# A chunked delta recurrence on one core: key and beta in one 128-row tile, state and outputs as products over 128 stacked rows, and the values' part of the right-hand side taken a chunk ahead

## Chip, cores and metric

One Trainium2 chip, one core, one launch. The metric is the device time of the launch in microseconds, the median of several executions; lower is better.

## What is computed

A decoder layer for 1024 tokens of width 1024 in float32: an RWKV-7 group of 8 heads and an attention group of 8 heads side by side, then a mixing product, LayerNorm, a feed-forward part and LayerNorm. The change touches only the state recurrence of the RWKV group. Cut to what matters:

```python
def wkv7_scan(r, w, k, v, kk, a):
    def step(S, inp):                       # S: 8 heads x 64 x 64
        r_t, w_t, k_t, v_t, kk_t, a_t = inp
        sa = einsum('bhvk,bhk->bhv', S, -kk_t)
        S = (S * w_t[:, :, None, :] + sa[..., :, None] * (kk_t * a_t)[:, :, None, :]
             + v_t[..., :, None] * k_t[:, :, None, :])
        return S, einsum('bhvk,bhk->bhv', S, r_t)
    ...                                     # 1024 steps, one after the other
```

## The kernel before

The launch is a row of blocks, each ended by a barrier of all engines: input projection, attention (`mla`), recurrence (`rwkv_chunks`), and then one long block for the group's outputs, the mixing and the feed-forward part. The order of work on every engine is written out by hand; engines meet only at semaphores, and each engine and each DMA queue runs its instructions in the order of the code.

The recurrence goes over NC_ = 16 chunks of CH = 64 tokens. Within a chunk the 64 steps are solved at once. Eight heads lie as RT = 4 tiles (index c) of 128 partitions, two heads p = 0, 1 to a tile, head p on the partitions `own[p]` (0 to 63 or 64 to 127). So nearly every product is a 64x64 by 64x64 float32 matmul, issued for p = 0 and p = 1 in turn, 8 of them (4 pairs) for one matrix per head. For chunk n the steps on TensorE are:

- `first_product` and the second `product` (L1794): two products that finish the inverse of a triangular matrix, from tiles that SP loads (L1685, six DMAs of 64 KB per chunk). Between them ACT copies out (`product_out`, L1847), and after them DVE merges (`merged`, L1914).
- `scores_step` (L1757, L1760, L1763): undecayed key by kk, undecayed key by decayed r, beta by decayed r, 12 pairs. DVE masks them out of PSUM (`mask_step`, L1923 and L1925).
- `transposes` (L1776, L1779, L1788): beta, key and values turned to token rows by matmuls with a 64-wide identity, 12 pairs. ACT copies them out (`tokens_step`, L1863, L1864).
- `rhs_step` (L1706, L1709): right-hand side, values' part plus state's part summed in PSUM, 8 pairs; DVE copies it (`rhs_out`, L1900).
- `sa_step` (L1718): inverse by right-hand side, 4 pairs; ACT copies it to `u` (`u_step`, L1853).
- `state_step` (L1728, L1731): keys by values plus beta by `u`, 8 pairs; DVE adds and decays (`state_out`, L1904, L1908).
- `y_step` (L1739, L1742, L1745): three products summed in PSUM, 12 pairs; ACT copies out (`y_leave`, L1857).

ACT also makes the decays of the next chunks (`exp_step`), DVE the decayed r (`r_step`), POOL the undecayed key (L1977). Steps of chunk m that need no state run a chunk ahead, between those of chunk n = m - 1:

```python
def stage(m, chain, ahead):
    n, z = m - 1, m % 3
    if ahead and m > 1: first_product(m)
    if chain: rhs_step(n)
    if ahead and m: scores_step(m)
    if chain: sa_step(n)
    ...                                     # second product, transposes(m)
    if chain:
        state_step(n)
        y_step(n)
```

Beta, 2 MB for all tokens, is loaded whole into `beta_all` near the end of the attention block (L1099). SP's queue in the recurrence is: the first quarter of the values (L1673), the six tiles of chunks 1 and 2, then, behind `sa_step(0)`, three quarters of the values and the gate weights, then the tiles of chunk 3, and from there six tiles a chunk, each set behind the `sa_step` three chunks back.

## Time and profile before

| | us |
|---|---|
| median of 3 runs | 1356.23 (1355.48 to 1357.2) |
| the profiled execution, its own time | 1353.33 |
| its span, first to last instruction | 1351.5 |
| recurrence block, first matmul to the first matmul behind it | 470.95 to 605.57 |

In a profile, PE is TensorE's matmuls and PEld its weight loads, DVE is VectorE, ACT is ScalarE, POOL is GpSimd, SP the queue that issues DMAs. L12 is line 12 of the kernel. A float32 matmul of this kernel leaves two records; a pair (p = 0 and p = 1) leaves four. A matmul's record lasts longer than the matmul keeps the engine, since neighbours overlap: pace is read from the starts. "x16" is a count of records; the name in square brackets behind a row is what ended the engine's idle time before it.

### The profile page before, as it was taken

The numbers are of one execution on the slowest core, as the hardware profiler recorded it, in microseconds if no ns is written. First come the engines' busy times: TensorE is split into PE (matmuls) and PEld (weight loads), VectorE is DVE, ScalarE is ACT, GpSimd is POOL, SyncE is SP. The second block draws the span as 40 slices with busy tenths as digits, with TensorE's granted clock in tenths as the row PEclk, the third lists the DMA queues.
The fourth block names the chain that finished last, engine by engine and source line by source line (L and its number), as shares of the span: only waits on it lengthen the run. The fifth ranks groups of instructions, "written<-read, shape, count | busy, mean of one in ns | idle before, by whom it ended". The sixth has DMA issues, their size and how long they took to land.

```text
span 1351.5 us, 23894 instructions
## 1 busy us (share of the span) xinstructions
PE 1315.0 (97%) x9900; PEld 1071.2 (79%) x9900; DVE 945.5 (70%) x1110; ACT 474.8 (35%) x796; POOL 497.0 (37%) x323
## 2 busy tenths in 40 slices
PE   7999999999999989989999999999999999999997
PEld 6877677877776789986688878888888888888886
DVE  3657975257777634439677988877777787669877
ACT  3143643146555433334104522212222444333330
POOL 0000112001876210002084778766774354444030
PEclk9999999999999999999999999999999999999999
DMA  5111444779639952224222345444436986666562
GB/s 225 62 48 32 141 157 156 184 169 292 183 101 288 221 127 53 59 64 140 87 101 94 117 137 198 142 147 164 156 125 226 356 288 219 190 198 200 190 205 106
DMA packets 147372, 214.50 MB, mean 159 GB/s; under 512 B 79960, under 2 KB 86240, under 8 KB 146624
## 3 DMA queue, kind: packets, MB, share of 16 engines
q1 hardware_dynamic: 146976, 211.92, 49.3%
q8 instruction: 79, 1.29, 0.4%
q10 hardware_dynamic: 288, 1.05, 0.2%
q14 instruction: 29, 0.24, 0.1%
HBM read 137.89 MB, written 66.39 MB: 151 GB/s over the span
## 4 chain that ended last, share of the span: by engine, by line
PE 49%; DVE 3%; POOL 1%; issue 1%; ACT 1%; DVEq 0%; POOLq 0%; ACTq 0%
PE banks L2523 23%; PE banks L2410 18%; PE banks L2326 5%; PE banks L2398 2%; POOL tile_h L3083 1%; PE banks L2371 1%; DVE wout_lo L2736 0%; POOL tile_s L3083 0%; DVE y_all L2756 0%; DVE first_relu L2870 0%; PE banks L2352 0%; DVE gn_scale L2747 0%; PE banks L156 0%; PE banks L2337 0%; DVE yr_full L2762 0%
## 5 line engine op out<-in xcount | busy, mean ns | idle before, releaser
L2523 PE MATMUL banks<-stage_b_hi,stage_a_hi 128*128 128x512 f32 x448 | 174.3, 389 | 0.0
L2523 PE MATMUL banks<-stage_b_lo,stage_a_hi 128*128 128x512 f32 x448 | 174.3, 389 | 0.0
L2523 PE MATMUL banks<-stage_b_hi,stage_a_lo 128*128 128x512 f32 x448 | 174.3, 389 | 0.0
L2898 DVE TENSOR_TENSOR stage_a_lo<-stage_a_raw,stage_a_hi 128x1024 fp32r<-128x1024 f32 x56 | 97.7, 1745 | 35.2 <-ACT stage_a_hi L2665 35.2
L2665 ACT ACTIVATE stage_a_hi<-stage_a_raw 128x1024 fp32r<-128x1024 f32 x56 | 59.4, 1061 | 120.9 <-DMA stage_b_raw<-in_w_ffn 98.4
L2523 PEld LDWEIGHTS banks<-stage_b_lo,stage_a_hi 128*128 128x128 f32 x448 | 84.1, 188 | 17.6
L2523 PEld LDWEIGHTS banks<-stage_b_hi,stage_a_hi 128*128 128x128 f32 x448 | 84.1, 188 | 17.4
L2523 PEld LDWEIGHTS banks<-stage_b_hi,stage_a_lo 128*128 128x128 f32 x448 | 84.1, 188 | 17.3
L852 POOL TENSOR_TENSOR hT<-hT,rate 128x1024 f32<-128x1024 f32 x4 | 13.5, 3370 | 210.1 <-DVE kk_tile L773 210.1
L428 PE MATMUL banks<-xT_hi,win_hi 128*128 128x512 f32 x288 | 90.6, 396 | 0.0
L428 PE MATMUL banks<-xT_lo,win_hi 128*128 128x512 f32 x288 | 88.8, 389 | 0.0
L428 PE MATMUL banks<-xT_hi,win_lo 128*128 128x512 f32 x288 | 88.7, 389 | 0.0
L1347 ACT ACTIVATE probs<-banks,neg_row_max 128x512 f32<-128x512 f32 (+1 forms) x96 | 55.3, 581 | 63.9 <-DVE neg_row_max L1442 38.9
L1439 DVE TENSOR_REDUCE row_max_parts<-banks 128x1 f32<-128x512 f32 (+1 forms) x96 | 50.6, 552 | 33.1 <-PE banks L1212 17.8
L428 PEld LDWEIGHTS banks<-xT_hi,win_hi 128*128 128x128 f32 x288 | 53.1, 188 | 19.4 <-issue 8.2
L3107 POOL TENSOR_TENSOR w_slots<-stage_b_raw,w_slots 128x1024 f32<-128x1024 f32 x16 | 45.6, 2856 | 52.9 <-DMA stage_b_raw<-in_w_ffn 48.3
L428 PEld LDWEIGHTS banks<-xT_lo,win_hi 128*128 128x128 f32 x288 | 54.1, 188 | 11.4
L428 PEld LDWEIGHTS banks<-xT_hi,win_lo 128*128 128x128 f32 x288 | 54.1, 188 | 11.3
L2901 DVE TENSOR_TENSOR stage_b_lo<-stage_b_raw,stage_b_hi 128x1024 fp32r<-128x1024 f32 x34 | 53.5, 1574 | 0.4
L1225 PE MATMUL banks<-ident,probs 128*128 128x128 f32 x288 | 48.4, 287 | 4.6 <-ACT late_probs_t L1359 2.5
L1977 POOL TENSOR_TENSOR k_undecayed<-hT,undecay 128x256 f32<-128x256 f32 x15 | 11.1, 743 | 108.3 <-ACT undecay L1841 108.3
L2883 DVE SCALAR_TENSOR_TENSOR tile_h<-tile_h 128x512 f32<-128x512 f32 x56 | 47.6, 849 | 1.4
(423 smaller groups left out, 3590.1 us busy)
## 6 DMA issues: line engine op xcount, KB each, us to landing
stage_b_raw<-in_w_ffn SPq DMA_DIRECT2D x50, 512.0 KB, 5.0
stage_a_raw<-hid_s SPq DMA_DIRECT2D x32, 512.0 KB, 4.0
w_landed<-in_w_ffn SPq DMA_DIRECT2D x30, 512.0 KB, 4.7
hid_s<-tile_s SPq DMA_DIRECT2D x60, 256.0 KB, 4.4
stage_a_raw<-hid_h SPq DMA_DIRECT2D x24, 512.0 KB, 4.0
hid_h<-tile_h SPq DMA_DIRECT2D x42, 256.0 KB, 2.0
win_raw<-in_w_in SPq DMA_DIRECT2D x20, 512.0 KB, 3.6
x_tok<-in_x SPq DMA_DIRECT2D x8, 512.0 KB, 7.6
```

What stands on the lines that cost most here:

```text
L428: last = mm(ps[:, 2 * j + b, :], w[j][:, kt, :], r[:, kt, b * HALF:(b + 1) * HALF], start=kt == 0 and i == 0, stop=kt == KT - 1 and i == 2)
L1225: last = nc.tensor.transpose(ps[:, BANK_T + u % 2, j * P:(j + 1) * P], probs[n % 3][:, j * P:(j + 1) * P], ident[:])
L1347: A_(probs[n % 3][:, 0:width], ps[:, u % 4, 0:width], ACT.Exp, bias=bias[:, qt:qt + 1], scale=SCALE, accum_out=sums[:, m, qt:qt + 1]).then ...
L1439: step.mark(V.reduce_max(tops[:, m, qt:qt + 1], ps[:, u % 4, 0:blocks_of(i, u) * P], AX_X))
L2326: last = nc.tensor.matmul(ps[:, bank + b, :], a[:, kt % RT, tok], w[:, kt, b * HALF:(b + 1) * HALF], start=kt == W_ORDER[0] and n == 0, st ...
L2410: last = nc.tensor.matmul(ps[:, bank_of(u, name), :], a[:, j, cut], b(kt), start=kt == 0 and n == 0, stop=kt == HK - 1 and n == 2)
L2523: last = nc.tensor.matmul(ps[:, bank, :], s[a][:, j, tok], s[b][:, j, :], start=p == 0 and j == 0 and n == 0, stop=p == NP - 1 and j == 1 ...
L2665: A(s["a_hi"][:], s["a_raw"][:], COPY).then_inc(hi2, 1)
L2883: V.scalar_tensor_tensor(hid[name][:], hid[name][:], 0.0, hid[name][:], ALU.max, ALU.mult).then_inc(hid_done, 1)
L2898: V.tensor_tensor(s["a_lo"][:], s["a_raw"][:], s["a_hi"][:].bitcast(F32), ALU.subtract).then_inc(lo2, 1)
L2901: V.tensor_tensor(s["b_lo"][:], src, s["b_hi"][:].bitcast(F32), ALU.subtract).then_inc(lo2, 1)
L3107: G.tensor_tensor(dst, a, b, ALU.subtract).then_inc(combined, 1)
```

## The change

Key and beta now lie in one tile `kb` of 128 partitions x 4 x 2 x 64. Four 128x128 transposes turn both for both heads of a tile at once (L1799 of the changed kernel); in the turned tile `kb_tok` the 64 token rows of the key lie on partitions 0 to 63 and those of beta on 64 to 127. In the same way `vu` holds the values' token rows on partitions 0 to 63 and the solved `u` on 64 to 127, and `rb` the scores of key and of beta by r. So `state_step` is one product over 128 stacked rows per head (8 matmuls of 128x64 weights), and so is the part of `y_step` that comes from values and `u`; the part from the old state stays a 64x64 product, into another bank, and DVE adds the two (`y_sum`), after ACT has copied one. The values' part of the right-hand side becomes `base_step(m)`, run at the end of the stage before; ACT copies it out (`base_out`), and `rhs_out` on DVE becomes an addition of it and the state's part. For the rows to stack, the score, `sa` and value-transpose products of the two heads now write the same 64 output partitions in two neighbouring banks. `beta_all` and its load are gone; chunk 0's beta (128 KB) is loaded in the attention block instead, and SP loads 128 KB of beta for each chunk behind that chunk's six tiles, and the three late quarters of the values also wait for `y_step(0)`. The core of the diff:

```diff
-    bk_tok = new("bk_tok", [P, 2, RT, CH], copies=2)
-    v_tok = new("v_tok", tile, copies=2)
-    u = new("u", tile)
+    kb_tok = new("kb_tok", [P, RT, 2, CH], copies=2)
+    vu = new("vu", [P, 2, RT, CH], copies=2)
...
-    own = (slice(0, 64), slice(64, P))
-    B, K, A_, R = 0, 1, 0, 1
-    B_SA, B_RY, B_T1, B_X, B_KS, B_B, B_BKT, B_V = range(8)
-    Y0 = RT
+    own = key_rows, beta_rows = (slice(0, 64), slice(64, P))
+    B_RY, B_TX, B_SC, _, B_VU, _, B_KB, B_ST = range(8)
+    K, B = 0, 1
+    Y0 = X0 = A0 = RT
     cols = lambda c: slice(c * CH, (c + 1) * CH)
     view = lambda bank, n=RT, at=0: ps[:, bank, at * CH:(at + n) * CH].rearrange("p (c n) -> p c n", n=CH)
+    by_head = lambda bank, rows=slice(0, P), at=0: ps[rows, bank:bank + 2, at * CH:(at + RT) * CH]
...
+                    sp.wait_ge(y_mm, 1)
...
+                if m >= 2:
+                    sp.wait_ge(tr_done, m - 1)
+                sp.dma_start(kb[m % 2][:, :, B, :], k.beta_d[:, :, now(m)]).then_inc(beta_in[m % 2], 16)
...
         def _(pe):
             mm = nc.tensor.matmul
 
-            def rhs_step(n):
-                q, a = n % 2, n % 3
+            def base_step(n):
+                q = n % 2
                 pe.wait_ge(sc_ready, n + 1)
                 pe.wait_ge(v_ready, n + 1)
-                pe.wait_ge(state_ready, n + 1)
-                if n >= 1:
-                    pe.wait_ge(y_out, n)
                 for c in range(RT):
                     for p in range(2):
-                        mm(ps[own[p], B_RY, cols(c)], ks[q][own[p], c, A_, :], v_tok[q][own[p], c, :],
-                           start=True, stop=False)
+                        last = mm(ps[own[p], B_SC, cols(c)], ka[q][key_rows, p, c, :], vu[q][key_rows, p, c, :],
+                                  start=True, stop=True)
+                last.then_inc(base_mm, 1)
+
+            def rhs_step(n):
+                q = n % 2
+                pe.wait_ge(state_ready, n + 1)
+                for c in range(RT):
                     for p in range(2):
-                        last = mm(ps[own[p], B_RY, cols(c)], kk_all[own[p], c, now(n)], state[q][own[p], c, :],
-                                  start=False, stop=True)
+                        last = mm(ps[own[p], B_ST, cols(A0 + c)], kk_all[own[p], c, now(n)], state[q][own[p], c, :],
+                                  start=True, stop=True)
                 last.then_inc(rhs_mm, 1)
 
             def sa_step(n):
                 pe.wait_ge(rhs_ready, n + 1)
                 pe.wait_ge(xt_up, n + 1)
+                if n >= 1:
+                    pe.wait_ge(part_ready, n)
                 for c in range(RT):
                     for p in range(2):
-                        last = mm(ps[own[p], B_SA, cols(c)], inv_t[n % 3][own[p], c, :], rhs[own[p], c, :],
+                        last = mm(ps[beta_rows, B_VU + p, cols(c)], inv_t[n % 3][own[p], c, :], rhs[own[p], c, :],
                                   start=True, stop=True)
                 last.then_inc(sa_mm, 1)
 
...
                 pe.wait_ge(sa_ready, n + 1)
                 for c in range(RT):
                     for p in range(2):
-                        mm(ps[own[p], B_SA, cols(c)], bk_tok[q][own[p], K, c, :], v_tok[q][own[p], c, :],
-                           start=True, stop=False)
-                    for p in range(2):
-                        last = mm(ps[own[p], B_SA, cols(c)], bk_tok[q][own[p], B, c, :], u[own[p], c, :],
-                                  start=False, stop=True)
+                        last = mm(ps[own[p], B_ST, cols(c)], kb_tok[q][:, c, p, :], vu[q][:, p, c, :],
+                                  start=True, stop=True)
                 last.then_inc(s_mm, 1)
 
             def y_step(n):
                 q, a = n % 2, n % 3
+                if n >= 1:
+                    pe.wait_ge(y_out, n)
                 for c in range(RT):
                     for p in range(2):
-                        mm(ps[own[p], B_RY, cols(Y0 + c)], state[q][own[p], c, :], rd[a][own[p], c, :],
-                           start=True, stop=False)
+                        mm(ps[own[p], B_RY, cols(c)], vu[q][:, p, c, :], rb[q][:, p, c, :], start=True, stop=True)
+                if n < NC_ - 1:
+                    pe.wait_ge(v_ready, n + 2)
+                for c in range(RT):
                     for p in range(2):
-                        mm(ps[own[p], B_RY, cols(Y0 + c)], v_tok[q][own[p], c, :], ks[q][own[p], c, R, :],
-                           start=False, stop=False)
-                    for p in range(2):
-                        last = mm(ps[own[p], B_RY, cols(Y0 + c)], u[own[p], c, :], bs[q][own[p], c, :],
-                                  start=False, stop=True)
+                        last = mm(ps[own[p], B_VU, cols(Y0 + c)], state[q][own[p], c, :], rd_of(n)[own[p], c, :],
+                                  start=True, stop=True)
                 last.then_inc(y_mm, 1)
 
             def scores_step(m):
                 q, a = m % 2, m % 3
                 if m >= 1:
                     pe.wait_ge(kd_ready, m)
+                    pe.wait_ge(beta_in[q], 16 * ((m + 1) // 2))
                     pe.wait_ge(rd_ready, m)
                     pe.wait_ge(sc_ready, m)
+                    pe.wait_ge(base_ready, m)
                 for c in range(RT):
                     for p in range(2):
-                        mm(ps[own[p], B_KS, cols(2 * c + A_)], kd[q][own[p], c, :], kk_all[own[p], c, now(m)],
+                        mm(ps[key_rows, B_SC + p, cols(A0 + c)], kb[q][own[p], c, K, :], kk_all[own[p], c, now(m)],
                            start=True, stop=True)
                     for p in range(2):
-                        mm(ps[own[p], B_KS, cols(2 * c + R)], kd[q][own[p], c, :], rd[a][own[p], c, :],
+                        mm(ps[key_rows, B_SC + p, cols(c)], kb[q][own[p], c, K, :], rd_of(m)[own[p], c, :],
                            start=True, stop=True)
                     for p in range(2):
-                        last = mm(ps[own[p], B_B, cols(c)], beta[own[p], c, now(m)], rd[a][own[p], c, :],
+                        last = mm(ps[beta_rows, B_SC + p, cols(c)], kb[q][own[p], c, B, :], rd_of(m)[own[p], c, :],
                                   start=True, stop=True)
                 last.then_inc(scores_mm, 1)
 
             def transposes(m):
                 q = m % 2
+                if m == 0:
+                    pe.wait_ge(centred, 1)
+                if m == 1 or m and m % 4 == 0:
+                    pe.wait_ge(v_in[m // 4], 16)
                 if m >= 1:
                     pe.wait_ge(tok_ready, m)
                 else:
...
                     pe.wait_ge(early_left, 1)
                 for c in range(RT):
                     for p in range(2):
-                        mm(ps[own[p], B_BKT, cols(B * RT + c)], beta[own[p], c, now(m)], k.eye[own[p], :],
-                           start=True, stop=True)
-                    for p in range(2):
-                        mm(ps[own[p], B_BKT, cols(K * RT + c)], kd[q][own[p], c, :], k.eye[own[p], :],
-                           start=True, stop=True)
-                if m == 0:
-                    pe.wait_ge(centred, 1)
-                if m == 1 or m and m % 4 == 0:
-                    pe.wait_ge(v_in[m // 4], 16)
+                        v = hT[own[p], T_V + c, now(m)] if m else k.first_v[own[p], c, :]
+                        mm(ps[key_rows, B_VU + p, cols(c)], v, centre[own[p], :], start=True, stop=True)
                 for c in range(RT):
-                    for p in range(2):
-                        v = hT[own[p], T_V + c, now(m)] if m else k.first_v[own[p], c, :]
-                        last = mm(ps[own[p], B_V, cols(c)], v, centre[own[p], :], start=True, stop=True)
+                    last = nc.tensor.transpose(ps[:, B_KB, c * P:(c + 1) * P],
+                                               kb[q][:, c, :, :].rearrange("p a n -> p (a n)"), ident[:])
                 last.then_inc(tr_done, 1)
 
...
+                pe.wait_ge(xt_up, m)
+                product(B_TX, low_t[z], inv[z]).then_inc(t1_mm, 1)
...
+                if ahead:
+                    base_step(m)
...
             def u_step(n):
                 act.wait_ge(sa_mm, n + 1)
-                if n >= 1:
-                    act.wait_ge(y_mm, n)
-                A(u[:], view(B_SA), ACT.Copy).then_inc(sa_ready, 1)
+                A(vu[n % 2][beta_rows, :, :, :].rearrange("p a c n -> p a (c n)"), by_head(B_VU, beta_rows), ACT.Copy)\
+                    .then_inc(sa_ready, 1)
 
             def y_leave(n):
                 act.wait_ge(y_mm, n + 1)
-                A(y_all[:, :, now(n)], view(B_RY, at=Y0), ACT.Copy).then_inc(y_out, 1)
+                if n >= 1:
+                    act.wait_ge(y_out, n)
+                A(y_part[:], view(B_VU, at=Y0), ACT.Copy).then_inc(part_ready, 1)
+
+            def base_out(n):
+                act.wait_ge(base_mm, n + 1)
+                if n >= 1:
+                    act.wait_ge(rhs_ready, n)
+                A(base[:], view(B_SC), ACT.Copy).then_inc(base_ready, 1)
 
             def tokens_step(m):
                 act.wait_ge(tr_done, m + 1)
                 if m >= 2:
                     act.wait_ge(y_mm, m - 1)
-                A(v_tok[m % 2][:], view(B_V), ACT.Copy).then_inc(v_ready, 1)
-                A(bk_tok[m % 2][:].rearrange("p a c n -> p (a c) n"), view(B_BKT, 2 * RT), ACT.Copy)\
-                    .then_inc(tok_ready, 1)
-
-            A(k.att_q[0][:], ps[:, B_BKT, :], ACT.Copy).then_inc(late_left, 1)
+                A(vu[m % 2][key_rows, :, :, :].rearrange("p a c n -> p a (c n)"), by_head(B_VU, key_rows), ACT.Copy)\
+                    .then_inc(v_ready, 1)
+                A(kb_tok[m % 2][:].rearrange("p c a n -> p (c a n)"), ps[:, B_KB, :], ACT.Copy).then_inc(tok_ready, 1)
...
             def rhs_out(n):
                 dve.wait_ge(rhs_mm, n + 1)
+                dve.wait_ge(base_ready, n + 1)
                 if n >= 1:
                     dve.wait_ge(sa_mm, n)
-                V.tensor_copy(rhs[:], view(B_RY)).then_inc(rhs_ready, 1)
+                V.tensor_tensor(rhs[:], base[:], view(B_ST, at=A0), ALU.add).then_inc(rhs_ready, 1)
...
+            def y_sum(n):
+                dve.wait_ge(part_ready, n + 1)
+                V.tensor_tensor(y_all[:, :, now(n)], y_part[:], view(B_RY), ALU.add).then_inc(y_out, 1)
...
-                both = mask[:].rearrange("p (o n) -> p o n", o=1).to_broadcast([P, RT, P])
-                until = mask[:, CH:P].rearrange("p (o n) -> p o n", o=1).to_broadcast([P, RT, CH])
-                V.tensor_tensor(ks[q][:].rearrange("p c a t -> p c (a t)"),
-                                ps[:, B_KS, :].rearrange("p (c n) -> p c n", n=P), both, ALU.mult)
-                V.tensor_tensor(bs[q][:], view(B_B), until, ALU.mult).then_inc(sc_ready, 1)
+                ahead = mask[key_rows, 0:CH].rearrange("p (o i n) -> p o i n", o=1, i=1).to_broadcast([CH, 2, RT, CH])
+                until = mask[:, CH:P].rearrange("p (o i n) -> p o i n", o=1, i=1).to_broadcast([P, 2, RT, CH])
+                V.tensor_tensor(ka[q][key_rows, :, :, :],
+                                by_head(B_SC, key_rows, A0).rearrange("p a (c n) -> p a c n", n=CH), ahead, ALU.mult)
+                V.tensor_tensor(rb[q][:], by_head(B_SC).rearrange("p a (c n) -> p a c n", n=CH), until, ALU.mult)\
+                    .then_inc(sc_ready, 1)
```

TensorE, the end of one chunk's stage in the steady part, before: from the value transposes to the next chunk's right-hand side. `bk_tok` are the turned keys and betas, `hT` holds the values.

```order
L1788 MATMUL banks<-centre,hT 64x64 x7
L1728 MATMUL banks<-v_tok_5313,bk_tok_5311 64x64 [waits d_sa_ready,d_tok_ready]
L1728 MATMUL banks<-v_tok_5313,bk_tok_5311 64x64
L1731 MATMUL banks<-u_5314,bk_tok_5311 64x64 x2
...
L1739 MATMUL banks<-r_decayed_2246,state_5316 64x64 x2
L1742 MATMUL banks<-k_scores_5301,v_tok_5313 64x64 x2
L1745 MATMUL banks<-b_scores_5303,u_5314 64x64 x2
...
L1794 MATMUL banks<-inverse_5307,low_t_5309 64x64 [waits d_base_in2]
L1794 MATMUL banks<-inverse_5307,low_t_5309 64x64 x7
L1706 MATMUL banks<-v_tok_5312,k_scores_5300 64x64 [waits d_state_ready,d_y_out,d_v_ready,d_sc_ready]
```

The same place of the changed kernel, with the waits of each step:

```order
L1797 MATMUL banks<-centre,hT 64x64 x7
L1799 MATMUL banks<-ident,k_and_beta_2247 128x128 x4
L1744 MATMUL banks<-vu_5313,kb_tok_5311 64x64 [waits d_sa_ready,d_tok_ready]
L1744 MATMUL banks<-vu_5313,kb_tok_5311 64x64 x7
L1754 MATMUL banks<-y_scores_5303,vu_5313 64x64 [waits d_y_out]
L1754 MATMUL banks<-y_scores_5303,vu_5313 64x64 x7
L1759 MATMUL banks<-r_decayed_5297,state_5315 64x64 [waits d_v_ready]
L1759 MATMUL banks<-r_decayed_5297,state_5315 64x64 x7
L1714 MATMUL banks<-vu_5312,k_scores_5300 64x64 [waits d_v_ready,d_sc_ready]
L1714 MATMUL banks<-vu_5312,k_scores_5300 64x64 x7
```

Sixteen matmuls of the state become eight, twenty-four of the outputs sixteen, and the values' part of the next right-hand side has moved to the end of the stage, behind the copies of the value transposes and of the scores.

SP's queue at the start of the recurrence in the changed kernel:

```order
L1678 DMA hT<-v_d 128x4x256
L1691 DMA inverse_t_5304<-inv_t_d 64x4x64 x2
L1691 DMA inverse_5306<-inv_d 64x4x64 x2
L1691 DMA low_t_5308<-low_d 64x4x64 x2
L1695 DMA k_and_beta_5296<-beta_d 128x4x64
...
L1695 DMA k_and_beta_2247<-beta_d 128x4x64 [waits d_tr_done]
L1678 DMA hT<-v_d 128x4x256 [waits d_y_mm,d_sa_mm]
L1678 DMA hT<-v_d 128x4x256 x2
L1688 DMA gate<-in_gate_g 128x512
L1691 DMA inverse_t_2240<-inv_t_d 64x4x64 x2
```

Before, the L1695 rows are not there, and the first of the three late value loads waits for `sa_step(0)` alone. Chunk 1's beta now stands behind chunk 1's six tiles, and chunk 3's tiles stand behind three value loads that wait for the outputs of chunk 0.

## Rows read from the trace of the kernel before

**Rows 1.** The page: busy time and share of the span per engine.
```profile
PE 1315.0 (97%) x9900; PEld 1071.2 (79%) x9900; DVE 945.5 (70%) x1110; ACT 474.8 (35%) x796; POOL 497.0 (37%) x323
```
**Rows 2.** Windows: length, busy us of PE, PEld, DVE, ACT, POOL, granted clock, DMA share, GB/s.
```profile
540.00:560.00 20.00, 19.70 (x660) 19.38 (x657) 9.55 (x22) 7.52 (x20) 1.59 (x3) 1.00 0.27 59
546.12:553.90 7.78, 7.68 (x263) 7.57 (x259) 3.62 (x9) 2.63 (x7) 0.73 (x1) 1.00 0.25 55
```
**Rows 3.** Timeline of TensorE, one steady chunk: start, length, what.
```profile
543.18 0.33 PE L1706 MATMUL banks<-v_tok,k_scores 64*64 64x64 f32 x4
...
544.13 0.31 PE L1757 MATMUL banks<-kk_all,k_undecayed 64*64 64x64 f32 x4
...
545.53 0.66 PE L1718 MATMUL banks<-rhs,inverse_t 64*64 64x64 f32 x16
...
550.99 0.33 PE L1706 MATMUL banks<-v_tok,k_scores 64*64 64x64 f32 x4
```
**Rows 4.** Groups within 470 to 606: busy us, mean ns, idle before.
```profile
L1923 DVE TENSOR_TENSOR k_scores<-banks,mask 128x512 f32<-128x512 f32 x16 | 11.1, 692 | 16.6 <-PE banks L1763 16.6
L1864 ACT ACTIVATE bk_tok<-banks 128x512 f32<-128x512 f32 x16 | 9.5, 592 | 0.0
L1853 ACT ACTIVATE u<-banks 128x256 f32<-128x256 f32 x16 | 6.1, 384 | 35.7 <-PE banks L1718 35.7
```
**Rows 5.** Timeline of TensorE elsewhere: tiles of other shapes, and changes between shapes.
```profile
172.11 2.08 PE L485 MATMUL banks<-kk_tile,beta_tile 64*64 64x64 f32 x64
174.12 1.13 PE L156 MATMUL banks<-key_norms,head_rows 32*128 32x512 f32 x4
...
460.19 0.65 PE L1260 MATMUL banks<-verse_sums_diagonal,ones_full 128*64 128x256 f32 x4
...
650.21 1.88 PE L2352 MATMUL banks<-hT,gate 128*128 128x512 f32 x4
```
**Rows 6.** A group of TensorE over the span: busy us, mean ns.
```profile
L466 PE MATMUL banks<-hT,w_lora 64*128 64x512 f32 x32 | 7.9, 615 | 0.0
```
**Rows 7.** The chain: sixteen 128x128 transposes on end.
```profile
707.96 1.75 PE banks L2371 x16
```
**Rows 8.** Timeline of SP's queue: the start of the recurrence, and one later pair.
```profile
470.92 0.56 SPq L1673 DMA_DIRECT2D hT<-v_d  x1
...
481.59 1.97 SPq L1673 DMA_DIRECT2D hT<-v_d  x3
...
487.25 1.68 SPq L1685 DMA_DIRECT2D low_t<-low_d  x2
...
534.04 2.68 SPq L1685 DMA_DIRECT2D low_t<-low_d  x2
```
**Rows 9.** Landing times of L1685: over all, and of the set issued from 484 on.
```profile
DMA to landing us min/median/max: 2.2/2.8/6.0
```
```profile
DMA to landing us min/median/max: 4.7/5.1/6.0
```
**Rows 10.** Timeline of TensorE, chunk 1's scores and chunk 0's solve.
```profile
477.05 0.33 PE L1757 MATMUL banks<-kk_all,k_undecayed 64*64 64x64 f32 x4 [0.94 <-POOL k_undecayed L1977]
...
478.50 0.63 PE L1718 MATMUL banks<-rhs,inverse_t 64*64 64x64 f32 x16
```
**Rows 11.** An idle stretch of TensorE, and the windows around it.
```profile
428.90 0.65 PE L1260 MATMUL banks<-verse_sums_diagonal,ones_full 128*64 128x256 f32 x4 [2.13 <-DVE verse_sums_diagonal L1475]
```
```profile
425.00:430.00 5.00, 2.87 (x21) 1.71 (x20) 4.93 (x6) 0.00 (x0) 2.82 (x2) 1.00 1.01 368
430.00:435.00 5.00, 5.00 (x26) 4.26 (x25) 2.98 (x7) 3.88 (x12) 0.00 (x0) 0.66 1.24 169
```
**Rows 12.** Timeline of TensorE, the last chunks and the block behind.
```profile
593.71 0.66 PE L1718 MATMUL banks<-rhs,inverse_t 64*64 64x64 f32 x16
...
601.03 0.68 PE L1718 MATMUL banks<-rhs,inverse_t 64*64 64x64 f32 x16 [0.52 <-DVE rhs L1900]
...
605.57 0.67 PE L2337 MATMUL banks<-hT,ones_block 128*128 128x512 f32 x1 [0.73 <-PEq L1655]
```

57 lines of the change are left out of this document (34 added, 23 removed).

## Prediction

> **What bounds the kernel now.** The page comes first: TensorE is busy 97% of the span, VectorE 70% [rows 1]. The chain of waits comes second, and it starts only at the barrier behind the recurrence, so of this block the windows and TensorE's timeline must tell. In the steady part TensorE is busy 19.70 of 20 us at a granted clock of 1.00, the 2.4 GHz level, while VectorE is busy 9.55 and ScalarE 7.52; one chunk, 7.78 us long, has 7.68 us of TensorE [rows 2]. TensorE's order of work is the bound, and the recurrence is some 135 us of the span [rows 10, 12]. The timeline gives the price of its unit: the twelve pairs of the scores run from 544.13 to 545.53, 1.40 us, so a pair of 64x64 matmuls takes 117 ns, and the chunk runs from 543.18 to 550.99, 7.8 us [rows 3]. Its 64 pairs make 7.47 us. The remaining 0.3 us is a wait before the right-hand side, for ScalarE's copy of the last outputs.
>
> **The steady chunk.** The change removes pairs: state 8 to 4, outputs 12 to 8, transposes of key and beta 8 to none; the right-hand side stays at 8, now 4 and 4. So 64 pairs become 48, or 5.60 us. It adds four 128x128 transposes. Sixteen such, on end, take 1.75 us, 109 ns each [rows 7], so 0.44 us. It also makes TensorE change the shape of its tiles: 64x64, then 128x128 for key and beta, then 128x64 for the state and the first part of the outputs, then 64x64 again, three changes a chunk. Before this the block had none. Elsewhere one can be seen: the 64 records of the 64x64 products start at 172.11 and end 2.08 us later; the last starts a record's length before that (0.22: the 0.31 of four that start within 0.09 [rows 3]), at 173.97, and the next shape starts at 174.12, 0.15 us on where the pace inside would give 0.06 [rows 5]. That is 0.09 us. The first weights behind a change are not loaded ahead, which adds half a pair's time, some 0.055. I take 0.145 a change, 0.44 us a chunk. The sum is 5.60 + 0.44 + 0.44 = 6.47 us.
>
> Could pairs that are formed otherwise run otherwise? Three kinds are new. State and outputs pair two 128x64 tiles that share all input rows: the trace has four records of 128x64 by 256 columns in 0.65 us, where the same columns through whole 128x128 tiles one by one would need 1.88 / 2 = 0.94 [rows 5]; they run side by side. Scores, `sa` and value transposes now pair two tiles from different halves of the rows onto the same 64 outputs, in two banks. The lora products are of that kind (64 rows each, the same 128 outputs, two banks): 32 records of 512 columns in 7.9 us [rows 6], 0.25 each, against 1.88 / 4 = 0.47 for whole tiles [rows 5]; side by side too. No row has the base products' kind (the same 64 input rows, two halves of the outputs); between 0.47 us, as now, and 0.93, taken singly, I take 0.47, since it lies nearest the 128x64 case. Last, beta's scores now go to another half of the array than key's, so their four pairs may run beside key's. No row shows four 64x64 tiles at work at once. The scores then take 8 to 12 pairs, 0.93 to 1.40 us, and the chunk 6.0 to 6.47. I take the middle, and 0.05 us for small waits: **6.3 us a chunk**.
>
> The Trainium skill, "TensorE: Matmul & The Clock Gate", section "Back-to-back issue gap", gives small matmuls a floor of about 25 ns from start to start. By it the scores' 48 records would take 1.2 us, and the chunk would be 6.3 too, as an estimate by that page; but records that start together leave this floor in doubt here.
>
> **Is anything else longer than 6.3?** The other engines per chunk: VectorE has 3.6 us busy [rows 2]. The masks go from 512 + 256 to 512 + 512 elements a row, at most +0.35 where 512 take 0.69 [rows 4], and the addition of the outputs adds about 0.42, as 256 elements out of PSUM take on ScalarE 0.38: about 4.4. ScalarE's copies of values and `u` have 512 elements a row instead of 256, 0.59 for 0.38 [rows 4], and the copy of the base is new, 0.38: 2.6 + 0.4 + 0.4 = 3.4. The serial path of a chunk (state's part 0.47, addition 0.42, `sa` 0.47, copy 0.59, state 0.47 and a change of shape 0.15, two operations on VectorE 0.8, and some 0.2 from end to start at each of four TensorE steps) is about 4.2. All lie below 6.3. Of the new waits on TensorE, the one for the addition of the last outputs is over long before; the one for the values' copy, in the middle of `y_step`, comes 0.59 + 0.2 us behind transposes, with state and half of the outputs, 0.94, between: hidden, by 0.1 to 0.3 us. SP's queue takes 1.68 us to issue a pair of a chunk's loads, and once 2.68 [rows 8]: six loads 5.0 to 6.0. A seventh, at the 0.66 of a value load (1.97 for three), gives 5.7 to 6.7. It fits on average, and the queue works two chunks ahead, but its slack shrinks to nothing.
>
> Chunks 3 to 14 are twelve periods: 12 x (7.78 - 6.3) = **-17.8 us**.
>
> **The start.** Here the change costs. Chunk 1's beta is issued behind the value load and six tiles, from 470.92 on. In the kernel before, the chunk 2 set begins where the new load will stand, at about 476.3. With the median landing time of 2.8 [rows 9], and twice the bytes, it lands at 479.5; chunk 1's scores began at 477.05 and `sa` at 478.50 [rows 10]. So `sa_step(0)` moves to 480.7, +2.2, and TensorE idles some 4 us before it. Then `y_step(0)` ends about 4.9 us later, at 485.6: the pairs above plus one wait for ScalarE's product. Only then do the late values go out, which were issued at 481.59. Chunk 3's last tile was issued at 488.3 and landed 4.7 us or more later, at 493 [rows 8, 9], so 11.4 us behind the first of these values: now 497.1. Chunk 2's work ends near 492. So TensorE idles some 5 us there, and `sa_step(2)` falls at 499.3 against 497.2. What I can't exclude is the clock. Behind an idle stretch of 2.1 us in the attention block the granted clock was 0.66 over the next five microseconds, that is about 3.4 us at the 1.2 GHz level [rows 11]. Each of the two longer idle stretches may cost the same, 3.4 / 2 = 1.7 us if all of it falls on work, nothing if it falls on waiting. I take 2.5 for both. Start: 2.1 + 2.5 = **+4.6 us**, between 2 and 7.
>
> **The end.** From `sa_step(14)` to the next block's first matmul are 11.9 us now [rows 12]. Chunk 14's rest loses 12 + 4 pairs and gains transposes and changes; the last chunk keeps its serial path but has half the pairs in state and in the right-hand side, waits no longer for the copied outputs before it, and gets an addition, 0.42, and a longer copy, 0.2, at its end. I count **-2.3 us**, between -1.5 and -3. Dropping the 2 MB load in the attention block I cost at nothing: it is covered by the last head's matmuls.
>
> **Sum:** -17.8 + 4.6 - 2.3 = -15.5 us. The profiled execution, 1353.3, would become 1337.8. It stood 2.9 below the median, which the change leaves; the median 1356.2 becomes **1340.7 us**.
>
> **Rivals.** (1) SP's queue, with its seventh load, or the landing of beta sets the period in place of TensorE: for it speak the 6.7 us of a set with a slow pair, against it the two chunks of lead. At 6.9 us the steady part gives 12 x 0.88 = 10.6, and with start and end -8: 1348.4. TensorE would then wait at every scores step for a DMA. (2) Slower than before: pairs from two row halves onto the same 64 outputs take turns. That is twenty of the 48 pairs (scores, `sa`, value transposes). Each would cost 117 ns more, +2.3 on 6.47, a chunk of 8.8 us: 12 x 1.0 = +12, start +9, end -2: about +19, 1375. It decides from 56 ns a pair on, where it eats the 15.5. The lora rows speak against it, but their columns are eight times as many, so weights count for little there. (3) The change doesn't do what it says: fewer matmuls, but the same period because a chain of waits binds. The 4.2 us path above speaks against it: 1356, hardly more than a remnant.
>
> **The numbers.** The forecast with a period of 6.0 to 6.5 has 0.77; its own range is 1334 to 1346 (period 6.0 and start +2: -21.2 + 2.1 - 2.5 = -21.6; 6.47 and start +7: -15.7 + 7 - 2 = -10.7). Rival 1 has 0.13, rival 2 has 0.06, rival 3 has 0.02; 0.02 is left for something faster. The range reaches into rival 1: 1333.5 to 1348.6. A change of 0.2%, 2.7 us, is about what a measurement of this kernel can tell from none. Faster by more 0.91, within 0.03, slower 0.06.
>
> **What would show it.** In the steady part: `sa_step` every 6.0 to 6.5 us; four transposes 109 ns apart with 0.15 us on either side; beta's score records starting between key's if they run beside them. At the start: one idle stretch of TensorE before chunk 1's scores, ended by the beta load, and one before chunk 3's first product, ended by an SP load, each with a lower clock behind it. I am wrong if the pairs onto shared outputs start 117 ns apart one by one, if a DMA ends TensorE's waits in the steady part, or if the start costs nothing.

## Result, and the profile after

The changed kernel takes 1338.11 us (median of 4 runs, 1335.56 to 1338.68), the kernel before 1355.86 (4 runs, 1353.22 to 1357.2). The ratio is 0.9873, 95% interval 0.9858 to 0.9888: **17.7 us faster**, where 15.5 were forecast. The profiled execution took 1338.68 us, its span is 1336.9. The page of the changed kernel, TensorE's share, answers to [rows 1]:

```profile
PE 1292.5 (97%) x8940; PEld 1044.8 (78%) x8940; DVE 953.9 (71%) x1126; ACT 487.4 (36%) x812; POOL 498.5 (37%) x323
```

By the two profiled executions the difference of 14.6 us comes apart like this (`sa_step(n)` begins at L1734, before at L1718):

| stretch | before | after | difference | forecast |
|---|---|---|---|---|
| start of the span to `sa_step(2)` | 497.21 | 502.94 | +5.7 | +4.6 |
| `sa_step(2)` to `sa_step(14)`, twelve chunks | 96.50 | 77.88 | -18.6 | -17.8 |
| `sa_step(14)` to the next block's first matmul | 11.86 | 10.01 | -1.9 | -2.3 |
| from there to the end of the span | 745.9 | 746.1 | +0.1 | 0 |

**The steady part.** The windows (length, busy us of PE, PEld, DVE, ACT, POOL, granted clock, DMA share, GB/s) over 20 us and over the shortest chunk, against [rows 2]:

```profile
540.00:560.00 20.00, 18.66 (x610) 17.39 (x608) 13.67 (x30) 10.64 (x26) 2.18 (x3) 1.00 0.38 85
555.29:561.08 5.79, 5.79 (x208) 5.49 (x204) 4.23 (x9) 3.43 (x8) 0.73 (x1) 1.00 0.37 85
```

This chunk, from one `sa_step` to the next, takes 5.79 us and TensorE is busy in all of it; VectorE has 4.23 and ScalarE 3.43 of the forecast's 4.4 and 3.4. But over the 20 us TensorE is busy 18.66, where it was busy 19.70 before: a chunk is shorter than forecast, and now something interrupts it. TensorE's timeline of that chunk, against [rows 3]:

```profile
555.29 0.46 PE L1734 MATMUL banks<-rhs,inverse_t 64*64 64x64 f32 x10
555.53 0.27 PE L1806 MATMUL banks<-inverse_t,product 64*64 64x64 f32 x1
...
556.01 0.27 PE L1797 MATMUL banks<-centre,hT 64*64 64x64 f32 x2
...
556.62 0.65 PE L1799 MATMUL banks<-ident,k_and_beta 128*128 128x128 f32 x4
557.20 0.69 PE L1744 MATMUL banks<-vu,kb_tok 128*64 128x64 f32 x16
557.72 0.64 PE L1754 MATMUL banks<-y_scores,vu 128*64 128x64 f32 x16
558.28 0.62 PE L1759 MATMUL banks<-r_decayed,state 64*64 64x64 f32 x13
558.68 0.27 PE L1714 MATMUL banks<-vu,k_scores 64*64 64x64 f32 x1
...
559.15 0.27 PE L1806 MATMUL banks<-inverse,low_t 64*64 64x64 f32 x1
...
560.09 0.27 PE L1773 MATMUL banks<-kk_all,k_and_beta 64*64 64x64 f32 x1
...
560.21 0.27 PE L1779 MATMUL banks<-r_decayed,k_and_beta 64*64 64x64 f32 x2
560.25 0.22 PE L1776 MATMUL banks<-r_decayed,k_and_beta 64*64 64x64 f32 x1
560.25 0.22 PE L1773 MATMUL banks<-kk_all,k_and_beta 64*64 64x64 f32 x1
...
561.08 0.34 PE L1734 MATMUL banks<-rhs,inverse_t 64*64 64x64 f32 x6
```

Read it from start to start. The scores take 560.09 to 561.08, 0.99 us for twelve pairs that would fill 1.40: beta's records (L1779) begin between key's. `sa` and the second product, four pairs each, begin at 555.29 and 555.53, 0.24 us apart, not 0.47: `sa` writes one half of the outputs only, and the product starts in the half that is free. State to the first part of the outputs, both 128x64, is 0.52 us, four pairs. The three changes of shape stand out as time beyond the pace of the step before them (0.47 us for four pairs, 0.44 for four transposes 0.109 apart): 0.14 us before the transposes (556.01 to 556.62), 0.14 behind them (to 557.20) and 0.09 between the two halves of the outputs (557.72 to 558.28).

What interrupts it: TensorE's timeline shows, about every second chunk, a gap that ends on nothing the profile knows ("issue"):

```profile
516.57 0.51 PE L1806 MATMUL banks<-inverse_t,product 64*64 64x64 f32 x10 [0.48 <-issue]
...
529.63 0.39 PE L1734 MATMUL banks<-rhs,inverse_t 64*64 64x64 f32 x6 [0.90 <-issue]
...
562.72 0.27 PE L1806 MATMUL banks<-inverse_t,product 64*64 64x64 f32 x2 [0.66 <-issue]
...
575.20 0.27 PE L1734 MATMUL banks<-rhs,inverse_t 64*64 64x64 f32 x1 [0.82 <-issue]
```

The twelve chunks average 6.49 us: 5.79 and 0.70 that is lost. Before it was 8.04: 7.78 and 0.26. Followed from start to start, about 0.55 of the 0.70 are such stalls. Another 0.08 is the clock: the first of the twelve chunks took 6.73 us at a granted clock of 0.84. Some 0.03 are waits for VectorE: `sa_step(7)` and `sa_step(8)` came 0.33 and 0.08 us late, each 0.05 us behind the end of `rhs_out` (L1925), which had stood in VectorE's queue behind L1974, 0.68 us of work for the attention group's output. No DMA of the kernel ends a wait of TensorE in the steady part.

The wider work on the other engines, groups from 470 to 591 (columns as in [rows 4]):

```profile
L1952 DVE TENSOR_TENSOR k_scores<-banks,mask 64x512 f32<-64x512 f32 x16 | 10.9, 683 | 13.1 <-PE banks L1779 13.1
L1954 DVE TENSOR_TENSOR y_scores<-banks,mask 128x512 f32<-128x512 f32 x16 | 10.8, 673 | 0.0
L1866 ACT ACTIVATE vu<-banks 64x512 f32<-64x512 f32 x16 | 9.5, 593 | 23.4 <-PE banks L1734 23.4
```

Half as many partitions save nothing (683 ns on 64, 673 on 128); the columns count, as the forecast had it.

**The start.** TensorE's waits from 470 to 510 (total us, times, longest), and the queue of SyncE (SP) there, against [rows 8, 10]:

```profile
PE banks L1773 <- DMA k_and_beta<-beta_d: 3.6, 1, 3.6
...
PE banks L1806 <- DMA low_t<-low_d: 3.5, 1, 3.5
...
PE banks L1714 <- issue: 1.3, 1, 1.3
```

```profile
475.88 0.61 SPq L1695 DMA_DIRECT2D k_and_beta<-beta_d  x1
...
488.48 1.89 SPq L1678 DMA_DIRECT2D hT<-v_d  x3
...
494.41 1.27 SPq L1691 DMA_DIRECT2D low_t<-low_d  x2
```

Chunk 1's beta is issued at 475.88 and lets the scores begin at 478.61; the late values go out at 488.48 (before: 481.59), chunk 3's last tile starts behind them at some 495.1 and ends TensorE's second idle stretch at 499.62. The windows show what the clock does around the two:

```profile
470.00:480.00 10.00, 5.75 (x172) 5.32 (x174) 3.56 (x8) 3.55 (x9) 1.70 (x2) 0.89 0.50 127
480.00:490.00 10.00, 9.53 (x205) 8.77 (x201) 3.50 (x8) 3.46 (x9) 0.00 (x0) 0.60 0.17 39
490.00:500.00 10.00, 5.22 (x160) 4.64 (x154) 3.49 (x8) 2.79 (x7) 0.73 (x1) 0.91 0.93 243
500.00:510.00 10.00, 10.00 (x287) 9.70 (x288) 4.20 (x10) 4.42 (x11) 1.03 (x2) 0.75 0.40 89
```

A granted clock of 0.89, 0.60, 0.91 and 0.75 over ten microseconds each means 17 us at the 1.2 GHz level in all (2 x (1.1 + 4.0 + 0.9 + 2.5)).

### The profile page after: what moved, and what is told of

Read it like the earlier page. It is cut to its first block, busy times and chain, and to the rows that moved or that the text cites. A ratio compares the mean times of both kernels' runs of the same rounds, so it can differ in the third digit from the quotient of the medians.

```text
span 1336.9 us, 22059 instructions
## 1 busy us (share of the span) xinstructions
PE 1292.5 (97%) x8940; PEld 1044.8 (78%) x8940; DVE 953.9 (71%) x1126; ACT 487.4 (36%) x812; POOL 498.5 (37%) x323
## 4 chain that ended last, share of the span: by engine, by line
PE 50%; DVE 3%; POOL 1%; issue 1%; ACT 1%; DVEq 0%; POOLq 0%; ACTq 0%
PE banks L2555 23%; PE banks L2442 18%; PE banks L2358 5%; PE banks L2430 2%; POOL tile_h L3115 1%; PE banks L2403 1%; DVE wout_lo L2768 1%; POOL tile_s L3115 0%; DVE y_all L2788 0%; DVE first_relu L2902 0%; PE banks L2384 0%; DVE gn_scale L2779 0%; PE banks L156 0%; PE banks L2369 0%; DVE yr_full L2794 0%
## 5 line engine op out<-in xcount | busy, mean ns | idle before, releaser
L2930 DVE TENSOR_TENSOR stage_a_lo<-stage_a_raw,stage_a_hi 128x1024 fp32r<-128x1024 f32 x56 | 100.9, 1801 | 36.8 <-ACT stage_a_hi L2697 36.8
L2009 POOL TENSOR_TENSOR k_and_beta<-hT,undecay 128x256 f32<-128x256 f32 x15 | 11.2, 744 | 99.3 <-ACT undecay L1856 99.3
```

The source lines that it names most:

```text
L2930: V.tensor_tensor(s["a_lo"][:], s["a_raw"][:], s["a_hi"][:].bitcast(F32), ALU.subtract).then_inc(lo2, 1)
```

## Experiments

Times are medians of each kernel's timed runs, beside the kernel before on the same chip. "Shortest" is the shortest distance of two `sa` steps, which has no stall in it, "mean" the mean from `sa_step(2)` to `sa_step(14)`; both are from the trace of one run. The changed kernel, e1 to e3, e3 again, e8, e9 and e10 ran on one chip, e4 to e7 on another, where the kernel before took 1357.6 us against 1356.0 and 1355.4. So a time of e4 to e7 is set against e3 by its ratio; each ratio's interval is 2 to 3 us either way.

| kernel | shortest | mean | time, us | ratio to before (95%) |
|---|---|---|---|---|
| changed, again | 5.79 | 6.43 | 1336.5 | 0.9866 (0.9841 to 0.9891) |
| e1 beta first | 5.78 | 6.44 | 1335.5 | 0.9856 (0.9833 to 0.9879) |
| e2 values later | 5.78 | 6.48 | 1333.4 | 0.9847 (0.9823 to 0.9871) |
| e3 both | 5.78 | 6.56 | 1330.0 | 0.9816 (0.9792 to 0.9840) |
| e3 again | 5.78 | 6.45 | 1330.2 | 0.9813 (0.9793 to 0.9832) |
| e3 + y2 first | 6.30 | 7.18 | 1338.5 | 0.9861 (0.9839 to 0.9883) |
| e3 + beta apart | 6.13 | 6.70 | 1330.4 | 0.9798 (0.9778 to 0.9817) |
| e3 + transposes twice | 6.22 | 6.73 | 1335.0 | 0.9836 (0.9819 to 0.9853) |
| e3 + no tiles | 5.78 | 6.57 | 1328.7 | 0.9789 (0.9769 to 0.9809) |
| e3 + base in chain | 6.11 | 6.65 | 1331.9 | 0.9826 (0.9806 to 0.9847) |
| e3 + wide turning | 6.07 | 6.79 | 1339.3 | 0.9879 (0.9858 to 0.9899) |
| e3 + tiles first | 5.78 | 6.52 | 1331.5 | 0.9820 (0.9800 to 0.9839) |

### The start

The changed kernel once more, with three variants of SyncE's queue.

> The changed kernel once more, beside its three variants on the same chip, as their base line. Every theory expects 1338 us (1336.5 to 1339.5), sa of the first chunk at 480.2 us, two idle stretches of TensorE in the recurrence's start (3.8 us and 3.7 us) and two stretches at half the granted clock (10.2 us and 6.8 us). If the idle stretches or the half clock come at other places, what is said of them from one trace falls.

It came out at 1336.5. The idle stretches are the same (waits of 3.3 and 3.4 us), the clock isn't; its windows over the same forty microseconds:

```profile
470.00:480.00 10.00, 5.66 (x158) 4.78 (x157) 3.55 (x8) 3.54 (x9) 1.69 (x2) 0.95 0.47 120
480.00:490.00 10.00, 9.53 (x297) 9.09 (x291) 4.70 (x10) 4.38 (x10) 0.73 (x1) 0.88 0.37 94
490.00:500.00 10.00, 5.26 (x120) 4.69 (x115) 2.43 (x7) 2.84 (x8) 0.00 (x0) 0.81 0.77 209
500.00:510.00 10.00, 10.00 (x302) 9.46 (x298) 5.66 (x12) 4.27 (x10) 1.45 (x2) 0.85 0.41 91
```

That is 2 x (0.5 + 1.2 + 1.9 + 1.5) = 10 us at the lower level, not 17. So the idle stretch brings the lower clock, but for how long differs between executions of one kernel, and with it `sa_step(2)`: 32.5 us behind the recurrence's first matmul in one, 29.7 in the other (before: 26.3). The expectation's 10.2 and 6.8 us fell.

```diff
+            sp.dma_start(kb[1][:, :, B, :], k.beta_d[:, :, now(1)]).then_inc(beta_in[1], 16)
             values(0)
             for m in range(1, NC_):
...
                 if m >= 2:
                     sp.wait_ge(tr_done, m - 1)
-                sp.dma_start(kb[m % 2][:, :, B, :], ...)
+                    sp.dma_start(kb[m % 2][:, :, B, :], ...)
```

> Chunk 1's beta is loaded first in SyncE's queue instead of eighth. Theory (the beta's landing alone holds TensorE for the 3.84 us up to 478.61, and this idle stretch is what brings the half clock of 477.8 to 488.0): scores of chunk 1 start at 474.8, the next wait is for chunk 1's low_t, which lands one issue (0.66 us) later than now, at 478.4; idle about 1.5 us there, no or a much shorter stretch at half clock. TensorE gets to the second chunk's end 3.5 to 4 us earlier, all behind it as before: 1334.4 us. Rival 1 (the tiles of chunk 1 land too late anyway): under 1 us gained, 1337.5. Rival 2 (the half clock stays, since it doesn't come from this idle stretch): 1.5 to 2 us gained, 1336.3.

`sa_step(0)` moved from 9.45 to 6.38 us behind the first matmul, but `sa_step(2)` only from 29.7 to 27.6, since the wait for chunk 3's tiles grew to 3.9 us. Behind what was left of the first wait, 1.5 us for chunk 1's `low_t`, the clock did not fall. Time: 1.0 us less in the median, where 3.7 were expected. Part of what the first wait gave was paid back at the second.

```diff
-                if m == 3:
+                if m == 4:
+                    values(1)
+                if m == 5:
                     sp.wait_ge(y_mm, 1)
-                    for n in range(1, 4):
-                        values(n)
+                    values(2)
+                if m == 6:
+                    values(3)
                     sp.dma_start(k.gate[:], k.later).then_inc(gate_in, 16)
```

> Chunk 3's tiles no longer stand behind the late values and their wait for the first chunk's outputs: the values' second quarter goes behind chunk 3's set, the third behind chunk 4's with that wait, the last and the gate behind chunk 5's. Theory (the wait and the values' transfers alone hold back chunk 3's tiles, idle 3.70 us before 499.62, and this brings the half clock of 498.2 to 505.1): the idle stretch and the half clock behind it go, 3.7 + half of 6.8 = 7.1 us gained: 1331.0 us. Rival 1 (the half clock stays): 3.7 us gained, 1334.4. Rival 2 (chunk 3's tiles then wait in the queue behind chunk 2's, or the values come late for chunk 4): under 2 us gained, 1336.5 or more.

The idle stretch before chunk 3 is gone, and `sa_step(2)` is at 23.2 us, 6.5 less than in the changed kernel's second run. The median fell by 3.1; this one profiled run lost time at the end again, with a stall of 2.6 us at 575.1 and 13.7 us at the lower level behind it.

> Both changes of SyncE's queue together. Theory: the gains add up, 3.7 + 7.1 us, 1327.3 us, and the granted clock is 1.00 through the recurrence. Rival (one idle stretch and one loss of the clock remain wherever the queue is late, the two gains overlap): no better than the better of the two, 1331 us.

1330.0, and 1330.2 in a second measurement (below): **6.6 us faster than the changed kernel on the same chip** (its runs 1335.07 to 1338.11, these 1328.95 to 1330.78). That is less than the 9.2 expected over that run, but `sa_step(2)` is at 22.2 us, 4 us ahead of the kernel before. The clock isn't 1.00 all through: 0.83 from 480 to 490, 3.4 us at the lower level behind what is left of idle time:

```profile
PE banks L1810 <- DMA low_t<-low_d: 1.3, 1, 1.3
PE banks L1777 <- POOL k_and_beta L2013: 0.9, 1, 0.9
```

The start's +3.4 to +6.2 us was therefore the order of the loads, no part of the new computation. All further experiments go on from e3.

### The steady chunk

> The version with both changes of SyncE's queue once more, as base line for the three beside it. Every theory: 1330 us (1328.5 to 1331.5), shortest chunk period 5.79 us. The stalls of TensorE that are put down to its instructions are expected again at multiples of 256 TensorE instructions from one another; if they lie elsewhere, the theory of the instruction stream falls.

Time and period came out so; so did the places of the stalls (last section).

```diff
                 for c in range(RT):
                     for p in range(2):
-                        mm(ps[own[p], B_RY, cols(c)], vu[q][:, p, c, :], rb[q][:, p, c, :], ...)
-                if n < NC_ - 1:
-                    pe.wait_ge(v_ready, n + 2)
-                for c in range(RT):
-                    for p in range(2):
                         last = mm(ps[own[p], B_VU, cols(Y0 + c)], state[q][own[p], c, :], rd_of(n)[own[p], c, :], ...)
+                for c in range(RT):
+                    for p in range(2):
+                        last = mm(ps[own[p], B_RY, cols(c)], vu[q][:, p, c, :], rb[q][:, p, c, :], ...)
```

(the wait for `v_ready` then stands ahead of both)

> Over the version with both changes of SyncE's queue (1330.0 us, shortest chunk period 5.79 us): the outputs' two halves change places, so that each chunk has five changes of the tile shape on TensorE in place of three. Theory (a change of shape costs 0.15 us, as the step from L1754 to L1759 and the steps around L1799 show, and TensorE's own work sets the period): 2 x 0.15 = 0.3 us more in each chunk, shortest period 6.09 us, 16 chunks 4.8 us: 1334.8 us. Rival (what looks like the price of a change of shape is the end of the step before it, and costs nothing of its own): period 5.8 us, 1330 us.

The shortest period rose by 0.52 us, not 0.30, and the time by 8.5 us, by the ratio by some 6, where 4.8 were expected. TensorE's timeline there:

```profile
562.56 0.69 PE L1748 MATMUL banks<-vu,kb_tok 128*64 128x64 f32 x16
563.40 0.68 PE L1760 MATMUL banks<-r_decayed,state 64*64 64x64 f32 x16 [0.16 <-ACT vu L1889]
564.01 0.69 PE L1764 MATMUL banks<-y_scores,vu 128*64 128x64 f32 x16
```

L1748 to L1760 is 0.84 us, 0.47 of work, 0.15 for the change and 0.22 more, most of which is the wait for the values' copy, which loses its cover when the 64x64 half comes first. L1760 to L1764 is 0.61: 0.47 and 0.14. A change of shape costs 0.14 to 0.15 us. And the order in which the change puts the two halves is worth a wait of its own.

```diff
                         mm(ps[key_rows, B_SC + p, cols(c)], kb[q][own[p], c, K, :], rd_of(m)[own[p], c, :], ...)
+                for c in range(RT):
                     for p in range(2):
                         last = mm(ps[beta_rows, B_SC + p, cols(c)], kb[q][own[p], c, B, :], rd_of(m)[own[p], c, :], ...)
```

> Over the same version: beta's four pairs of scores follow key's eight in a loop of their own. Theory A (in the changed kernel beta's pairs run beside key's, four 64x64 tiles at once, so that 12 pairs take 0.99 us): the loop costs 0.41 us more in each chunk (1.40 us for the scores), shortest period 6.2 us, 16 chunks 6.2 to 6.6 us: 1336.4 us. Theory B (key's two products already run beside each other, whatever beta's do; or the records only overlap and the pairs take turns): period 5.8 us, 1330 us.

The shortest period rose by 0.35 us, and the scores' timeline shows why: key's two products now go in turn, in groups of four records 0.117 us apart, and beta's (L1784) follow from 559.14 on.

```profile
558.26 0.27 PE L1777 MATMUL banks<-kk_all,k_and_beta 64*64 64x64 f32 x1
...
558.49 0.33 PE L1780 MATMUL banks<-r_decayed,k_and_beta 64*64 64x64 f32 x4
558.61 0.33 PE L1777 MATMUL banks<-kk_all,k_and_beta 64*64 64x64 f32 x4
...
559.14 0.27 PE L1784 MATMUL banks<-r_decayed,k_and_beta 64*64 64x64 f32 x2
...
559.65 0.34 PE L1738 MATMUL banks<-rhs,inverse_t 64*64 64x64 f32 x6
```

558.26 to 559.65 is 1.39 us, against 0.99: theory A holds in the period. In the time it doesn't: 1330.4, as without the edit, and by the ratio some 2 us less, which the intervals can't tell from nothing. The longer chunk loses less to stalls (0.57 us a chunk; 0.67 and 0.78 in the two traces of e3), which gives back 0.10 to 0.21 of the 0.35 us; where the rest went is not shown.

```diff
-                for c in range(RT):
+                for c in (*range(RT), *range(RT)):
                     last = nc.tensor.transpose(ps[:, B_KB, c * P:(c + 1) * P], ...)
```

> Over the same version: the four 128x128 transposes are made twice over, onto the same outputs. Theory (TensorE's own work sets the period and a transpose costs 0.109 us): 4 x 0.109 = 0.44 us more, shortest period 6.23 us, 16 chunks 7.0 us: 1337.0 us. Rival (a chain of evictions sets 5.79 us, TensorE has slack): under 0.1 us per chunk, 1331 us at most.

Shortest period +0.44 us, to the hundredth what four transposes cost: TensorE's own work sets the chunk. The time rose by 5.0, by the ratio by some 3, not by 7.0; again stalls fell, to 0.51 us a chunk.

```diff
-                    pe.wait_ge(base_in[z], 96 * (m // 3 + (z > 0)))
+                    pe.wait_ge(base_in[z], 96 * (z > 0))
...
-                    for p in range(2):
+                    for p in range(2 if m < 3 else 0):
                         sp.dma_start(dst[m % 3][own[p], :, :], ...)
```

> Over the same version: the tiles of inverse_t, inverse and low_t are loaded for chunks 0 to 2 alone, and the later chunks compute with these. The stalls of 0.6 to 1.3 us that lift the mean period from 5.79 to 6.5 us lie 256, 512, 768, 1024 or 1280 TensorE instructions apart. Theory A (they are waits for TensorE's own instructions, and those come late because their transfers share the DMA engines with the tiles' 24,576 bytes in 256-byte pieces): the stalls go, mean period 5.8 us, 12 x 0.7 = 8 us gained: 1321.5 us. Theory B (instructions come late whatever else is moved): stalls as before, 1330 us. Theory C (SyncE's queue holds the chain somewhere, unseen): the shortest period falls under 5.79 us.

(A set is six loads of 64 KB; 24,576 bytes is a sixteenth of it, one DMA engine's share. This version leaves out the tiles' later loads, so what it computes is not the layer.) The shortest period stays 5.78: theory C is out, SyncE's queue holds nothing. The stalls stay too, mean 6.57. Two late ones at the same instructions were smaller (0.68 and 0.77 us from start to start at L1810 and L1738, where e3 had 1.31 and 1.04), an early one at L1810 was larger (1.3 us idle, in e3 1.0), and one of 3.1 came in at L1727:

```profile
PE banks L1727 <- issue: 2.9, 1, 2.9
PE banks L1810 <- issue: 1.8, 2, 1.3
PE banks L1738 <- issue: 1.1, 2, 0.6
```

The time fell by 1.3 us, by the ratio by some 3.5, not by 8. Theory A fails as the main cause; some share of the tiles' traffic is not excluded.

```diff
                 if chain:
+                    base_step(n)
                     rhs_step(n)
...
-                if ahead:
-                    base_step(m)
```

> Over that version: the values' part of the right-hand side is no longer a chunk ahead; its step stands right before rhs_step of the same chunk. TensorE's work is the same. Theory (the score's banks are then free only when ScalarE has moved the part out, 0.05 + 0.38 + 0.2 us after the step, of which rhs_step covers 0.47 us, so TensorE waits 0.2 to 0.4 us before the scores): shortest period 6.0 to 6.2 us, 15 chunks 3 to 6 us: 1334.5 us. Rival (rhs_step and the order of the banks cover it, the chunk ahead is worth nothing): 1330 us. Second rival (ScalarE's copy then queues behind other evictions and holds VectorE's right-hand side too): over 0.6 us per chunk, 1340 us or more.

Shortest period 6.11, +0.33 as the theory has it: that is what computing the values' part a chunk ahead is worth in a clean chunk. In time 1.8 us of the expected 4.4; the mean rose only by 0.1 to 0.2.

```diff
                 for c in range(RT):
-                    last = nc.tensor.transpose(ps[:, B_KB, c * P:(c + 1) * P], ...)
+                    for a, rows in enumerate(own):
+                        last = mm(ps[rows, B_KB, c * P:(c + 1) * P], kb[q][:, c, a, :], ident[:], start=True, stop=True)
```

> Over that version: key and beta are turned by eight plain products of 128 rows and 64 outputs against the 128 columns of the identity, in the tile shape of the state's products behind them, in place of four 128x128 transposes: one change of shape less (0.15 us), while the products (64 columns take 0.117 us a pair in L1748) take 0.21 to 0.23 us a pair, four pairs 0.88 us in place of 0.44. Theory (the sum of such terms sets the period): +0.44 - 0.15 = 0.29 us more, shortest period 6.08 us, 16 chunks 4.7 us: 1334.7 us. Rival (the 128x128 form costs more around it than the three changes of 0.15 us say): 1331 us or less.

Shortest period 6.07, +0.29 as expected to the hundredth: transposes, pairs and changes of shape add up. But the time rose by 9.2 us, not 4.7. Against the two traces of e3 the start grew by 3.5 to 4.0 us, the twelve chunks by 2.8 to 4.1 and the end by 1.1 to 2.8. In the twelve chunks the loss to stalls is no larger than in e3 (0.72 us a chunk). It is the stalls outside them: 1.7 us idle on "issue" ahead of `sa_step(2)`, where e3 has none, and a stall of 2.6 us at the end. With twelve more matmul records a chunk, stalls fall at other places; whether they fall there in every run of e9 one trace doesn't show.

```diff
-            values(0)
+            sp.dma_start(kb[1][:, :, B, :], k.beta_d[:, :, now(1)]).then_inc(beta_in[1], 16)
             for m in range(1, NC_):
...
+                if m == 1:
+                    values(0)
```

(with e2's edit beside it, as in e3)

> Over that version: the values' first quarter is loaded behind chunk 1's tiles, not ahead of them. The tiles are issued 0.66 us earlier and no longer share the engines with 256 KB of values. Theory (chunk 1's low_t, the last tile to land, holds TensorE for the 1.5 us after the first sa step): this idle stretch shrinks to under 0.5 us, 1.0 to 1.5 us gained, 1328.8 us. Rival (the values then land too late for the first value transposes, or other waits take its place): 1330 us or more.

A miss: 1331.5, and chunk 1's low_t still held TensorE for 1.7 us (1.3 and 1.9 in e3's traces). The values ahead of the tiles were not what made them late. The trace is of the slowest of six runs, 1338.0 us, with a stall of 2.4 us and 10.2 us at the lower clock at its end; the start, which is read here, doesn't have them.

## Why the prediction was right, and where it was not

**TensorE's order of work is the bound:** shown for a chunk without stalls, by e6 (+0.44 for 0.44) and by a clean chunk in which TensorE is busy 5.79 of 5.79 us. In the mean, 0.70 us of the 6.49 is something else.

**A chunk of 6.3 us.** Right in its sum, by two errors that offset. The pairs and the transposes cost what was said, and 0.145 for a change of shape was near (0.14, 0.14 and 0.09 in the clean chunk, 0.14 to 0.15 in e4; e9's sum). The step that failed upward is "the scores take 8 to 12 pairs; I take the middle": they took 0.99 us, the lower end, and e5 shows it is beta beside key. Not thought of at all was that whole steps overlap where one uses half of the outputs: `sa` and the second product, 0.23 us. 6.47 - 0.41 - 0.23 gives 5.83; 5.79 is measured. The step that failed downward is "0.05 us for small waits": 0.70 us a chunk is lost, most of it to the stalls on "issue". It was 0.26 a chunk before, and the forecast counted the period before as 7.78 and left the loss out on both sides. That the total still came within 0.8 us of -17.8 is luck: the stalls, nowhere in the sum, happened to take back most of what the overlaps gave. (The low end of the range has a slip besides: 12 x 1.78 is 21.4, not 21.2.)

The estimate by the Trainium skill ("TensorE: Matmul & The Clock Gate", section "Back-to-back issue gap", a floor of about 25 ns from start to start) gave the scores 1.2 us. The trace doesn't bear it out: 48 records in 0.99 us, 21 ns each, some 0.01 us apart.

**The start, +4.6.** Both waits came where they were put, ended by the loads that were named (3.6 and 3.5 us, forecast 4 and 5). `sa_step(2)` moved by 5.7 in one profiled run; measured from the recurrence's first matmul by 6.2 and 3.4 us in two. The term that was mis-sized is the clock: "Each of the two longer idle stretches may cost the same, 3.4 / 2 = 1.7 us", from 3.4 us at the 1.2 GHz level each. It was 10 to 17 us at that level for both together. On the forecast's own path it cost some 4 us in the first profiled run, where 2.5 were taken: the late values went out at 488.48 instead of 485.6, and `sa_step(2)` came 3.3 us behind the landing of chunk 3's last tile instead of 2.2. e3 takes the whole start term back and more: `sa_step(2)` is 3.5 to 4.0 us ahead of the kernel before.

**The end, -2.3:** -1.9. **The dropped 2 MB load, 0:** the recurrence's first matmul starts at 470.47 after 470.95, and in other runs at 470.2 to 473.5: nothing to be seen.

**The rivals.** (1) SyncE's queue sets the period: out, no DMA ends a wait there and e7 leaves the period at 5.78. (2) Pairs of two halves of the rows onto the same outputs take turns: out, `sa`'s and the values' pairs keep 0.11 to 0.12 us. (3) A chain of waits keeps the period: out, the shortest period fell by 1.99 us.

## What to carry to other kernels

A price list of TensorE's work (pairs, transposes, changes of shape, and which quarters of the array a step leaves free) gave the effect on a clean chunk within 0.06 us for four of the five edits to TensorE's work, and the fifth uncovered a wait. It did not give the time: 0.35 us more a chunk, on sixteen chunks, came out as nothing that the runs can tell in e5, and 0.29 as 9 us in e9. Where stalls fall into TensorE's stream, read the shortest period and the mean apart, and judge an edit by the timed runs. And when a load is cut up and put into a queue, look at what it stands behind in the first rounds: two moves in the order of the loads were worth 6.6 us, where the whole change was worth 17.7.
